# A hybrid decoder step on one core: memory K/V projected first, the SSD scan cut into items among dense tiles, key units among attention heads

## The chip, the cores and the metric

The kernel runs on one core of one Trainium2 chip. The metric is the device time of one execution in microseconds (us). Five engines work in parallel, each through its own list of instructions: TensorE (PE, matrix products and transposes), VectorE (DVE), ScalarE (ACT), GpSimd (POOL) and SyncE (SP, which here issues nearly all loads).

## What is computed

One step of one decoder layer, in fp32, with the same weights for a prompt of 256 tokens and for 32 sample tokens (8 sequences, 4 steps each); the kernel treats them as one matrix of 288 columns.

```python
def trunk_layer(h, l, q_start, conv_state, ssm_state, k_past, v_past, mem_k, mem_v, p):
    hn = rmsnorm(h, p['norm_mix'][l])
    proj = hn @ p['w_in'][l]                                  # 1024 x 4112
    z, xbc, dt_raw, q, k, v = jnp.split(proj, SPLIT_IDX, axis=-1)
    y_ssd, new_conv, new_ssm = ssd_branch(z, xbc, dt_raw, conv_state, ssm_state, ...)
    y_att = moba_attention(q, k_all, v_all, q_start, p['rel_bias'])
    h = h + jnp.concatenate([y_ssd, y_att], axis=-1) @ p['w_out'][l]
    h = h + cross_attend(rmsnorm(h, p['norm_ca'][l]), mem_k, mem_v, ...)
    hn = rmsnorm(h, p['norm_mlp'][l])
    h = h + jnp.square(jax.nn.relu(hn @ p['w_up'][l])) @ p['w_down'][l]
```

`ssd_branch` is a causal convolution over x, B and C with SiLU, a scan with 16 heads of 64 and a state of 128 (two chunks of 128 for the prompt, one chunk of 4 steps for each sample sequence, from its own stored state), a gate with SiLU(z) and a norm. `moba_attention` has 8 heads of 64; a query attends to its own block of 256 keys and to the three earlier blocks whose mean key scores highest. The sample's 1024 past keys and values per sequence are gathered from a pool by a page table. The memory's K/V (256 tokens) are projected from a normed memory input for the prompt, and read from a cache for the sample. Outputs are y of both groups and the new K/V, memory K/V, convolution and SSM states.

## The kernel before

**Tiles and blocks.** A dense projection is done in pairs of tiles: 128 output columns x 288 tokens each, 16 matmuls of one 128x128 weight tile (8 k-tiles, fp32) by 288 columns. A pair's weights are one block of 256 columns, 1 MB, in a ring of four slots (`wring`); `load_block` (L563) issues it. Tiles gather in PSUM banks 0 and 1 and are evicted by VectorE.

**Units.** The gathered cache comes in units of 2 MB, eight pages of 256 KB. `K(g,k)` and `V(g,k)` are four units for each of two groups g of four sequences. `kvring` has two slots, and `load_unit` (L587) issues one DMA a page in a register loop that reads the page number (L594 to L596). It first waits in `slot_free` until the unit two before is used. A K unit on TensorE is 32 transposes (L829) and 32 short products with the queries (L924); a V unit is 16 products (L945). `MK`/`MV` are the memory's cache units, `ST` the SSM states.

**Turns.** Every transpose into PSUM that is copied out again, and many small products, are "turns". `plan_turns` (L239) numbers them in program order over banks 2, 3 and 6 (`TURN_BANKS`); ScalarE and VectorE take them alternately. Each turn waits for the copy of the turn three before.

**The order.** `make_plan` (L109) writes one list, `SEQ`, by hand. All five engines walk the same list, each doing its own part of each item, and wait for one another by semaphores. SP walks it too, and does `load_block` at a pair and `load_unit` at a unit: one serial queue. Around the change it is: qk 0, sum of squares of x, `early` (eight transposes of the memory and its squares, the convolution history), qk 1, then K(0,0) to K(0,3) each with a pair (qk, v) behind it, own 0 (products of queries with the sample's new keys, followed by `self_bounds` on VectorE and `row_exps` on ScalarE), v 1, K(1,0), kvtok (K/V to token rows, stored), the memory's norm, four m pairs among K(1,1) to K(1,3), mtok; then `heads_in` (POOL loads the relative bias rows by DMA, VectorE adds them to the first scores), x pairs, V units and eight self heads, dt, z pairs. A head on TensorE is a product of scores (L969), a transpose of probabilities (L829) and a product with values (L980). Then a meeting of all engines, and `ssd()` alone: two prompt chunks (segments, outputs, new states), the sample's chunk with 16 state reads one by one (L1113) and 16 updates (L1132 on TensorE, L1942 on VectorE, four operations each). Then the output projection (8 k-tiles of the SSD part and 4 of the attention part, L864 and L866), caq (queries of the cross attention, L843 at 467.45 us), a meeting, the cross attention, its projection and the MLP.

**The start.** VectorE's first part makes the relative-bias tables and waits for all six table loads (`wait_ge(tab_in, 96)`) ahead of L1999. Only behind that does it evict the transposed x (L1646). SP issues the tables behind x, the vectors and weight block 0.

The lines that the prediction speaks of:

```python
            def load_block(key):
                g = BLOCK[key]
                if g >= SLOTS:
                    old = BLOCKS[g - SLOTS]
...
                    with sp.Fori(0, 8) as i:
                        page = sp.value_load(pages[0:1, ds(i + first, 1)], min_val=0, max_val=cache.shape[0] - 1)
                        sp.dma_start(big[:, ds(i * 512 + (n % 2) * 4096, 512)],
                                     cache[ds(page, 1)].rearrange("o p n -> p (o n)")).then_inc(kv_in[n % 2], 16)
```

## Time and profile before

| | |
|---|---|
| runs: median of 3 (lowest, highest) | 789.86 us (789.83, 791.85) |
| the profiled execution's own time | 791.33 us |
| its span in the profile | 789.5 us |
| mean granted TensorE clock | 0.950 of full speed |
| TensorE busy | 709.1 us (90%) |
| VectorE busy | 415.8 us (53%) |
| ScalarE busy | 142.0 us (18%) |
| POOL busy | 120.5 us (15%) |
| bytes moved | 126.18 MB, mean 160 GB/s |

The span is what the profile sees between the first and the last instruction; the own time has the launch around it. Times in the rows are from the span's start. "Busy" is the time an engine's instructions ran; matmuls are pipelined, so a busy TensorE is not one at its peak. The granted clock is a share of 2.4 GHz: at 0.5 TensorE runs at 1.2 GHz. In a timeline row, the brackets give the time for which the engine was idle before the row's first instruction, and the operation that released it.

### The profile page before, as it was taken

Reading aid. Unit: us, or ns where it says so; the run is one execution under the profiler, and the core shown is the slowest. Engines: PE = TensorE matmul, PEld = TensorE weight load, DVE = VectorE, ACT = ScalarE, POOL = GpSimd, SP = SyncE. Lnnn points to the kernel's source line nnn. Section 1 sums busy time; section 2 is a strip of 40 time slices with the busy share of each in tenths; the row PEclk is TensorE's granted clock in tenths of the full one; section 3 lists DMA queues with packets and bytes.
Section 4 is the critical chain, followed back from the end, with each engine's and each line's share of the span. In section 5 each row is a group of like instructions: output and inputs, shape, how many; then the busy total and the mean of one; then the engine's idle time right before and its main releaser. Section 6 shows DMA issues by size and latency. Waiting matters only on the chain. (4 is left out here: it accounts for less than half of the span.)

```text
span 789.5 us, 12071 instructions
## 1 busy us (share of the span) xinstructions
PE 709.1 (90%) x4351; PEld 543.4 (69%) x4351; DVE 415.8 (53%) x905; ACT 142.0 (18%) x322; POOL 120.5 (15%) x200
## 2 busy tenths in 40 slices
PE   4879999997999997889879997868999999999993
PEld 2456677785756674543326775537999999999992
DVE  2253244243876821884387222536788887445524
ACT  2131114222101021431111000411211111000002
POOL 3120001003002002200034110003254444000000
PEclk9969999999899999796979998989999999999998
DMA  9563677687779955400006790456354444544401
GB/s 285 135 178 100 207 241 254 224 264 210 220 232 288 294 142 138 137 1 1 1 0 165 235 320 0 147 174 213 108 159 145 145 150 152 186 161 161 160 1 61
DMA packets 102492, 126.18 MB, mean 160 GB/s; under 512 B 6385, under 2 KB 78565, under 8 KB 102440
## 3 DMA queue, kind: packets, MB, share of 16 engines
q1 hardware_dynamic: 99240, 115.08, 46.5%
q0 software_dynamic: 3200, 10.39, 4.6%
q8 instruction: 35, 0.57, 0.3%
q14 instruction: 17, 0.14, 0.1%
HBM read 117.14 MB, written 8.31 MB: 159 GB/s over the span
## 5 line engine op out<-in xcount | busy, mean ns | idle before, releaser
L843 PE MATMUL ps<-hw,wring 128*128 128x288 f32 x576 | 152.3, 426 | 5.7 <-DVE qs L1692 3.7
L843 PEld LDWEIGHTS ps<-hw,wring 128*128 128x128 f32 x576 | 114.5, 200 | 42.4 <-DVE qs L1692 4.1
L1646 DVE COPY tmp<-ps 128x512 f32<-128x512 f32 (+3 forms) x84 | 53.6, 643 | 67.3 <-PE ps L829 61.4
L829 PEld LDWEIGHTS ps<-ident,big 128*128 128x128 f32 x400 | 45.6, 146 | 37.2 <-issue 13.1
L829 PE MATMUL ps<-ident,big 128*128 128x128 f32 x400 | 58.6, 289 | 10.0 <-DVE tmp L1646 6.3
L1441 ACT ACTIVATE tmp<-ps 128x512 f32<-128x512 f32 (+4 forms) x71 | 39.7, 562 | 131.4 <-PE ps L829 111.3
L1239 PE MATMUL ps<-hw,wring 128*128 128x144 f32 x256 | 35.5, 294 | 2.2 <-DVE hw L1649 2.2
L709 POOL TENSOR_TENSOR acc<-acc,sq 128x288 f32<-128x288 f32 (+1 forms) x35 | 27.9, 798 | 52.9 <-ACT sq L1447 50.8
L1239 PEld LDWEIGHTS ps<-hw,wring 128*128 128x128 f32 x256 | 33.7, 196 | 2.7 <-DVE hw L1649 2.7
L1239 PE MATMUL ps<-big,wring 128*128 128x144 f32 x256 | 34.0, 286 | 0.0
L866 PE MATMUL ps<-big,wring 128*128 128x288 f32 x128 | 32.6, 408 | 0.5 <-DVE big L1649 0.5
L1239 PEld LDWEIGHTS ps<-big,wring 128*128 128x128 f32 x256 | 32.4, 190 | 0.0
L866 PEld LDWEIGHTS ps<-big,wring 128*128 128x128 f32 x128 | 24.2, 190 | 7.8 <-DVE big L1649 1.3
L843 PE MATMUL ps<-tmp,wring 128*128 128x256 f32 x128 | 28.5, 381 | 0.0
L924 PE MATMUL ps<-tmp,qs 128*32 128x256 f32 x320 | 25.6, 390 | 2.9 <-ACT tmp L1441 1.6
L758 POOL COPY attT<-ohT 64x16 f32<-64x16 f32 (+1 forms) x24 | 4.6, 194 | 150.6 <-ACT ohT L1441 141.8
L1595 ACT ACTIVATE xc<-ps 128x144 f32<-128x144 f32 x20 | 5.8, 288 | 119.5 <-PE ps L1239 119.5
L843 PEld LDWEIGHTS ps<-tmp,wring 128*128 128x128 f32 x128 | 24.1, 190 | 3.6 <-issue 0.4
L1602 ACT ACTIVATE big<-big 128x288 f32<-128x288 f32 x32 | 13.0, 444 | 74.2 <-DVE big L2113 74.2
L809 POOL TENSOR_TENSOR tmp<-big 128x144 f32<-128x144 f32 x16 | 15.9, 997 | 66.3 <-ACT big L1602 66.3
L829 PE MATMUL ps<-ident,tmp 128*128 128x128 f32 (+1 forms) x94 | 16.1, 304 | 10.0 <-DVE tmp L1772 4.7
L1239 PE MATMUL ps<-tmp 128*128 128x144 f32 x192 | 24.8, 286 | 0.0
(306 smaller groups left out, 1177.1 us busy)
## 6 DMA issues: line engine op xcount, KB each, us to landing
wring<-in_w_in SPq DMA_DIRECT2D x16, 1024.0 KB, 6.9
big<-in_cache_k SPq DMA_DIRECT2D x64, 256.0 KB, 2.7
big<-in_cache_v SPq DMA_DIRECT2D x64, 256.0 KB, 3.5
wring<-in_w_up SPq DMA_DIRECT2D x16, 1024.0 KB, 5.3
wring<-in_w_down SPq DMA_DIRECT2D x16, 1024.0 KB, 5.0
wring<-in_w_out SPq DMA_DIRECT2D x8, 768.0 KB, 8.7
wring<-in_w_ca_kv SPq DMA_DIRECT2D x4, 1024.0 KB, 5.3
big<-in_state_ssm SPq DMA_DIRECT2D x8, 512.0 KB, 6.1
```

Source lines behind the costliest of these rows:

```text
L709: pool.tensor_tensor(a, a, sq[:, m % 2, 0:n], ALU.add).then_inc(acc_done, 1)
L758: copy = pool.tensor_copy(dst, src)
L809: step(pool.tensor_tensor(ff_sums[:, 0, n], a[1], a[0], ALU.subtract))
L829: last = pe.transpose(ps[0:c, bank(key), col:col + r], in_, ident[0:r, 0:r])
L843: last = pe.matmul(ps[:, t % 2, 0:width], w, rhs(c * k_tiles + k), start=(c + k == 0), stop=(c == chunks - 1 and k == k_tiles - 1))
L866: last = pe.matmul(ps[:, t % 2, 0:T], w, z[:, k, :], start=(k == 6), stop=(k == 5))
L924: last = pe.matmul(ps[32 * b:32 * b + 32, bk, lo:lo + 256], qs[:, c, u[1] * GB + b, :], (xKT if cross else KT_)[:, step % 2, b, :], start= ...
L1239: last = pe.matmul(ps[:, bank_, col * HALF:(col + 1) * HALF], w(k), x(k), start=(start and k == 0), stop=(stop and k == 3))
L1441: act.activation(dst, src, ACT.Copy).then_inc(turn_act, 1)
L1595: act.activation(parts[:, u % 2, 0], ps[:, A, 0:HALF], ACT.Copy).then_inc(p1_made, 1)
L1602: act.activation(ff[:, c * T:(c + 1) * T], ff[:, c * T:(c + 1) * T], ACT.Square).then_inc(ff_done, 1)
L1646: dve.tensor_copy(dst, src).then_inc(turn_dve, 1)
```

## The change

It writes `SEQ` anew and adapts every engine's part to it. No product of the reference's is dropped.

- **Start**: the memory input, block x0, the convolution history and block m0 are issued by SP ahead of the tables. All engines first do the memory transposes (`memt`), the history (`hist`) and the tables (`tab`); VectorE's wait for the tables stays ahead of its x copies.
- **Dense part**: pairs of x and m come first, then dt, z, qk, v. The first m pair and the first x pair are held in PSUM until their norms are there (`HELD`).
- **Scan**: cut into `cv`, `tok`, `sums`, `seg`, `stt`, `yd`, `upd`, `ys`, `yo`, `sst`, the sample's chunk first (`CHUNKS = [2, 0, 1]`), most of them between single z, qk and v tiles. The state reads go four at a time. The square norm of y (`zsq`), `state` and the drain `over` stand between the K units.
- **Units**: K(0,0) follows all dense tiles but those of the output. The eight K units stand among seg, yo, kvtok, zsq, own, probs and heads 0 to 3; the V units among heads 4 to 7 and the SSD part of the output projection (`oz`). The attention part (`oa`) follows the last V unit. `load_unit(n + 2)` is issued at unit n.
- **Evictions**: some turns get a fixed engine (`EVICTOR`, `PLACE_OF`). Shared buffers replace some copies. One of the two meetings is gone.
- POOL loads the bias rows at `heads_in` only behind the drain; ScalarE's `zsq` waits for two K/V stores to land, since it writes where their source is.

The core of the diff:

```diff
-    pair("qk", 0, 1)
-    item("ss", 0)
-    item("early")
-    pair("qk", 1, 1)
+    item("memt")
+    item("hist")
+    item("tab")
+    pair("x", 0)
+    pair("m", 0)
+    item("ss", "x")
+    pair("x", 1)
+    item("ss", "mem")
+    pair("m", 1)
...
     unit("K", 0, 3)
+    item("heads_in", "self")
     item("own", 0)
-    pair("v", 1, 1)
     unit("K", 1, 0)
-    item("kvtok")
-    item("ss", 1)
-    pair("m", 0, 1)
+    item("ss", "ssd")
+    item("head", "self", 0)
     unit("K", 1, 1)
     item("probs", 0)
-    pair("m", 1, 1)
+    item("head", "self", 1)
...
-            load_block(BLOCKS[0])
+            sp.dma_start(memin, I["mem_prompt"].rearrange("(g p) n -> p g n", p=P)).then_inc(mem_in, 16)
+            load_block(0)
+            sp.dma_start(cvin, I["state_conv"]).then_inc(cv_in, 16)
+            load_block(1)
...
             for s in SEQ:
-                if s[0] == "pair":
-                    for c in range(s[3]):
-                        if BLOCK[s[1:3] + (c,)] >= done:
-                            load_block(s[1:3] + (c,))
-                elif s[0] == "unit":
-                    load_unit(s[1:])
...
+                elif s == ("seg", 0, 1):
+                    load_unit(2)
+                elif s == ("seg", 0, 3):
+                    load_unit(3)
+                elif s[0] == "unit" and s[1] != "ST" and UNIT[s[1:]] + 2 < len(UNITS):
+                    load_unit(UNIT[s[1:]] + 2)
...
                 elif s == ("heads_in", "self"):
-                    in_ps(pool, ("mvtok", 1))
+                    pool.wait_ge(ssd_over, 2)
+                    in_ps(pool, ("sf", 1))
                     pool.wait_ge(rb_out, 16)
                     load_bias(0), load_bias(1)
...
+                elif s[0] == "stt":
+                    for k in range(0, 20, 4):
+                        if k < 16:
+                            for i in range(k, k + 4):
+                                state_turn(i)
+                        if k == 4:
+                            pe.wait_ge(cz_made, 1)
+                        if k >= 4:
+                            for i in range(k - 4, k):
+                                turned(pe, ("state", i))
+                            for i in range(k - 4, k):
+                                state_read(i)
...
+                elif s[0] == "zsq":
+                    act.wait_ge(y_used, 4 + s[1] + 1)
+                    act.wait_ge(kst_out[0], 16)
+                    act.wait_ge(kst_out[2], 16)
+                    for c in (2 * s[1], 2 * s[1] + 1):
+                        square("ssd", c, z[:, c, :], T)
```

How the instructions move, at three places. SP at the start, before (the tables are the rows from rb to mask_p):

```order
L614 DMA vec_rows<-in_conv_w 48x128
L572 DMA wring<-in_w_in 128x8x256
L616 DMA rb<-in_rel_bias 128x1x8
L617 DMA rb_tab<-in_rel_bias 32x8
L618 DMA step_of<-in_step_of 128x4
L619 DMA big<-in_onehot_s 128x1056
L620 DMA wring<-in_onehot_p 32x512
L621 DMA wring<-in_mask_p 8x512
L622 DMA big<-in_mem_prompt 128x2x1024
L623 DMA mkv<-in_state_conv 24x1536
L572 DMA wring<-in_w_in 128x8x256 x2
```

and in the change:

```order
L743 DMA vec_rows<-in_conv_w 48x128
L744 DMA tmp<-in_mem_prompt 128x2x1024
L701 DMA wring<-in_w_in 128x8x256
L746 DMA mkv<-in_state_conv 24x1536
L701 DMA wring<-in_w_ca_kv 128x8x256
L748 DMA rb<-in_rel_bias 128x1x8
L749 DMA rb_tab<-in_rel_bias 32x8
L750 DMA step_of<-in_step_of 128x4
L751 DMA big<-in_onehot_s 128x1056
L752 DMA wring<-in_onehot_p 32x512
L753 DMA wring<-in_mask_p 8x512
L701 DMA wring<-in_w_in 128x8x256
```

The memory, the history and a second weight block now stand ahead of the tables.

TensorE at own 0, before (L843 a dense pair, L829 and L924 the next K unit, behind L1216, own 0):

```order
L843 MATMUL ps<-hw,wring 128x288 x16
L829 MATMUL ps<-ident,big 128x128 x16
L924 MATMUL ps<-tmp,qs 32x256 x4
L829 MATMUL ps<-ident,big 128x128 x8
L924 MATMUL ps<-tmp,qs 32x256 x4
L829 MATMUL ps<-ident,big 128x128 x8
L924 MATMUL ps<-tmp,qs 32x256 x8
```

and in the change (L976 and L1046 are the K units' transposes and products, L1088 the first two scores of the heads, L1338 own 0):

```order
L976 MATMUL ps<-ident,big 128x128 x8
L1046 MATMUL ps<-tmp,qs 32x256 x8
L1088 MATMUL ps<-kT,qz 128x256 x4
L1338 MATMUL ps<-kT,qs 32x32 x16
L976 MATMUL ps<-ident,big 128x128 x16
L1046 MATMUL ps<-tmp,qs 32x256 x4
L976 MATMUL ps<-ident,big 128x128 x8
L1046 MATMUL ps<-tmp,qs 32x256 x4
```

The dense pair between own 0 and K(1,0) is gone, and two score products of the heads stand ahead of own 0.

TensorE at the end of the V units, before (L945 a V unit, L843 dense tiles, L980, L829 and L969 a head, L954 pvend):

```order
L945 MATMUL ps<-big,tmp 32x512 x8
L843 MATMUL ps<-hw,wring 128x288 x16
L980 MATMUL ps<-tmp,vtok 64x256 x2
L829 MATMUL ps<-ident,tmp 128x128 x4
L969 MATMUL ps<-kT,qz 128x256 x2
L843 MATMUL ps<-hw,wring 128x288 x16
L945 MATMUL ps<-big,tmp 32x512 x8
L980 MATMUL ps<-tmp,vtok 64x256 x2
L829 MATMUL ps<-ident,tmp 128x128 x4
L843 MATMUL ps<-hw,wring 128x288 x32
L945 MATMUL ps<-big,tmp 32x512 x8
L954 MATMUL ps<-vtok,tmp 32x512 x4
```

and in the change (L1067 a V unit, L1017 dense tiles, L1107 and L976 a head, L1076 pvend):

```order
L1067 MATMUL ps<-big,tmp 32x512 x8
L1017 MATMUL ps<-big,wring 128x288 x8
L1107 MATMUL ps<-tmp,vtok 64x256 x2
L976 MATMUL ps<-ident,tmp 128x128 x4
L1067 MATMUL ps<-big,tmp 32x512 x16
L1107 MATMUL ps<-tmp,vtok 64x256 x2
L1067 MATMUL ps<-big,tmp 32x512 x8
L1076 MATMUL ps<-vtok,tmp 32x512 x4
L976 MATMUL ps<-ident,tmp 128x128 x4
L1017 MATMUL ps<-big,wring 128x288 x8
L1017 MATMUL ps<-attT,wring 128x288 x32
```

Before, the three L945 rows are V(1,1) to V(1,3), with four dense pairs and two heads among them. In the change the rows of L1067 are V(1,0) to V(1,3): one dense tile and one head stand ahead of V(1,1) and V(1,2), which follow one another (x16), and one product of the last head ahead of V(1,3). The attention part of the output stands behind.

## Rows read from the trace of the kernel before

**Rows 1.** Busy time by stretch: us, each engine's busy time (instructions), clock, DMA share, GB/s.
```profile
0.00:60.00 60.00, 40.08 (x129) 25.17 (x130) 20.50 (x43) 14.75 (x38) 14.95 (x25) 0.89 0.68 197
60.00:311.00 251.00, 240.74 (x1476) 170.00 (x1474) 118.08 (x262) 49.08 (x108) 18.19 (x43) 0.99 0.71 215
311.00:419.50 108.50, 90.13 (x389) 42.56 (x388) 71.99 (x162) 27.75 (x52) 13.86 (x31) 0.84 0.13 39
419.50:467.50 48.00, 47.45 (x197) 36.72 (x196) 18.50 (x40) 5.67 (x11) 13.85 (x17) 1.00 0.83 263
467.50:549.00 81.50, 65.09 (x351) 45.08 (x349) 34.27 (x74) 18.17 (x47) 7.86 (x16) 0.92 0.41 137
549.00:774.00 225.00, 222.36 (x1794) 221.50 (x1794) 146.05 (x318) 20.71 (x55) 50.15 (x65) 0.99 0.43 138
774.00:789.50 15.50, 3.21 (x24) 2.38 (x24) 6.37 (x10) 5.89 (x12) 1.63 (x3) 0.75 0.21 77
```

**Rows 2.** Timeline of the start: start us, us, engine, line, operation [idle before, releaser].
```profile
13.27 0.29 DVE L1999 TENSOR_TENSOR wring<-rb,step_of 128x128 f32<-128x128 f32 x1 [13.27 <-DMA wring<-in_mask_p]
...
26.29 10.29 PE L843 MATMUL ps<-hw,wring 128*128 128x288 f32 x32 [2.00 <-DVE wring L2012]
...
38.24 1.95 DVE L1726 RECIPROCAL rstd<-rstd 128x288 f32<-128x288 f32 x1 [0.60 <-ACT rstd L1539]
...
45.67 1.41 PE L829 MATMUL ps<-ident,big 128*128 128x128 f32 x4 [0.59 <-DVE tmp L1646]
...
47.76 1.44 PE L829 MATMUL ps<-ident,mkv 24*128 24x24 f32 x12 [0.69 <-DVE tmp L1646]
...
49.14 10.81 PE L843 MATMUL ps<-hw,wring 128*128 128x288 f32 x32
```

**Rows 3.** Busy time by stretch, two short stretches.
```profile
8.00:22.00 14.00, 10.71 (x29) 5.40 (x30) 6.56 (x13) 6.28 (x14) 5.97 (x8) 1.00 1.07 335
...
495.00:515.00 20.00, 17.01 (x154) 10.47 (x154) 11.46 (x24) 8.29 (x24) 0.00 (x0) 1.00 0.51 178
```

**Rows 4.** Timeline, K(0,0) and its next dense pair; own 0's bounds beside a pair.
```profile
59.78 1.47 PE L829 MATMUL ps<-ident,big 128*128 128x128 f32 x12
...
67.21 8.03 PE L843 MATMUL ps<-hw,wring 128*128 128x288 f32 x32
...
111.19 8.03 PE L843 MATMUL ps<-hw,wring 128*128 128x288 f32 x32
...
111.60 1.23 DVE L1737 TENSOR_REDUCE small<-ps 128x4 f32<-128x1024 f32 x1
...
119.62 0.18 ACT L1460 ACTIVATION_READ_ACCUMULATOR tmp<-tmp,small 128x1 f32 x1
```

**Rows 5.** Timeline of the heads and V units.
```profile
182.89 2.17 POOL L721 DMA_DIRECT2D tmp<-bias_rows  x4
...
192.03 0.69 DVE L1963 SCALAR_TENSOR_TENSOR tmp<-ps,tmp 128x512 f32<-128x512 f32 x1 [10.73 <-DMA tmp<-bias_rows]
...
211.03 10.83 SPq L596 DMA_DIRECT2D big<-in_cache_v  x8
...
212.35 7.92 PE L843 MATMUL ps<-hw,wring 128*128 128x288 f32 x32
...
220.20 1.92 PE L945 MATMUL ps<-big,tmp 128*32 128x512 f32 x16
```

**Rows 6.** Timeline of the scan: transposes, two state reads, the updates.
```profile
359.74 2.79 PE L829 MATMUL ps<-ident,big 128*128 128x128 f32 x12 [0.28 <-issue]
...
372.14 1.05 PE L1113 MATMUL ps<-tmp 128*32 128x512 f32 x2
...
373.70 1.04 PE L1113 MATMUL ps<-tmp 128*32 128x512 f32 x2
...
400.42 18.35 PE L1132 MATMUL ps<-tmp 128*128 128x512 f32 x28 [3.43 <-DVE big L1942]
```

**Rows 7.** DMA issues: tile and source, operation, count, KB each, median us to landing.
```profile
big<-in_cache_v SPq DMA_DIRECT2D x64, 256.0 KB, 3.5
```

More of the change, by code:

```diff
@@ L110, in make_plan, with pair, tile @@
     seq = []
-    def pair(kind, n, chunks):
-        seq.append(("pair", kind, n, chunks))
+    def pair(kind, n):
+        seq.append(("tile", kind, n, 0))
+        seq.append(("tile", kind, n, 1))
+    def tile(kind, n, half):
+        seq.append(("tile", kind, n, half))
     def unit(*a):
@@ L119, in item @@
         seq.append(a)
-    pair("qk", 0, 1)
-    item("ss", 0)
-    item("early")
-    pair("qk", 1, 1)
-    unit("K", 0, 0)
-    pair("qk", 2, 1)
-    unit("K", 0, 1)
-    pair("qk", 3, 1)
+    item("memt")
[7 more added lines that the diff above has]
+    pair("m", 1)
+    pair("x", 2)
+    unit("ST", 0)
+    unit("ST", 1)
+    pair("m", 2)
+    pair("x", 3)
+    pair("m", 3)
+    pair("x", 4)
+    item("mtok")
@@ new lines, in make_plan @@
+    pair("x", 5)
+    item("dt")
+    tile("z", 0, 0)
+    item("dt_series")
+    tile("z", 0, 1)
+    item("dt_rates")
+    tile("z", 1, 0)
+    item("silu_x")
+    tile("z", 1, 1)
+    tile("z", 2, 0)
+    item("cv")
+    item("tok", 2)
+    tile("z", 2, 1)
+    item("sums", 2)
+    tile("z", 3, 0)
+    item("seg", 2, 0)
+    item("stt")
+    tile("z", 3, 1)
+    item("silu_z")
+    item("yd")
+    item("upd", 0, 2)
+    tile("qk", 0, 0)
+    item("ys")
+    item("upd", 2, 6)
+    tile("qk", 0, 1)
@@ new lines, in make_plan @@
+    item("upd", 6, 10)
+    item("tok", 0)
+    tile("qk", 1, 0)
+    item("upd", 10, 14)
+    tile("qk", 1, 1)
+    item("upd", 14, 16)
+    item("sums", 0)
+    tile("qk", 2, 0)
+    item("seg", 0, 0)
+    tile("qk", 2, 1)
+    item("seg", 0, 1)
+    item("yo", 0, 0)
+    tile("qk", 3, 0)
+    item("seg", 0, 2)
+    item("yo", 0, 1)
+    tile("qk", 3, 1)
+    item("seg", 0, 3)
+    item("yo", 0, 2)
+    tile("v", 0, 0)
+    item("yo", 0, 3)
+    item("sst", 0)
+    item("tok", 1)
+    tile("v", 0, 1)
@@ L129, in make_plan @@
+    item("sums", 1)
+    tile("v", 1, 0)
+    item("seg", 1, 0)
+    tile("v", 1, 1)
+    item("seg", 1, 1)
+    item("yo", 1, 0)
+    unit("K", 0, 0)
+    item("seg", 1, 2)
+    item("yo", 1, 1)
+    item("kvtok", 0, 2)
+    item("seg", 1, 3)
+    item("yo", 1, 2)
+    unit("K", 0, 1)
+    item("yo", 1, 3)
+    item("sst", 1)
+    item("kvtok", 2, 3)
+    item("zsq", 0)
+    item("zsq", 1)
     unit("K", 0, 2)
-    pair("v", 0, 1)
+    item("zsq", 2)
+    item("zsq", 3)
+    item("state")
+    item("over")
@@ L219 @@
     elif s[0] == "dt":
         TILE["dt"] = len(TILE)
-    elif s[0] == "unit" and s[1] in ("K", "V"):
-        UNIT[s[1:]] = len(UNIT)
-    elif s[0] == "ssd":
-        for h in range(2):
-            UNIT[("ST", h)] = len(UNIT)
     elif s[0] == "unit":
         UNIT[s[1:]] = len(UNIT)
-N_BLOCKS, N_TILES, N_USED = len(BLOCK), len(TILE), len(USED)
+N_BLOCKS, N_TILES = len(BLOCK), len(TILE)
+HELD = {("x", 0): "x", ("m", 0): "mem", ("caq", 0): "ca"}
+EVICT, BANK, IN_BANK = {}, {}, {}
+for s in SEQ:
+    if s[0] == "tile" and s[1:3] not in HELD:
+        EVICT[s[1:4]] = len(EVICT)
+    elif s[0] == "dt":
+        EVICT["dt"] = len(EVICT)
+    elif s[0] == "ss":
+        for kind, name in HELD.items():
+            if name == s[1]:
+                for half in range(2):
+                    EVICT[kind + (half,)] = len(EVICT)
@@ L1529, in _ @@
+            leave("vec")
+            for c in range(DT):
+                leave(("x", c))
+                turned(act, ("x", c))
+                square("x", c, h3[:, c, :], T)
             for s in SEQ:
```

1390 lines of the change are left out of this document (703 added, 687 removed).

## The prediction

> **What bounds the kernel now.** I read the busy time by stretches first [rows 1]: TensorE is busy for 709.07 us of the 789.50 us span (the sum of the seven rows), so the kernel is bound by TensorE, and what can change is its idle time and the time it spends at the lower of its two clock levels. Both are concentrated: 18.4 us idle in the scan stretch 311.00 to 419.50, with a mean granted clock of 0.84; 19.9 us idle in the first 60 us at 0.89; 16.4 us around the meeting before the cross attention; 12.3 us at the end. In 60 to 311, where every K or V unit is followed by dense tiles, only 10.3 of 251.0 us are idle. The DMA engines move 39 GB/s during the scan against 215 and 263 GB/s beside it. So spreading the scan among dense tiles could pay at most for what the scan stretch loses. But the dense tiles it uses are the ones that covered the K units and the page loads. The question is what is late next once that cover has moved. I walk TensorE's order from 0 to the start of caq0 at 467.45; behind it both orders are the same, and I leave its 322.05 us of span unchanged.
>
> **The start.** Today mask_p, the last table, lands at 13.27, and VectorE, which stands in a wait for it ahead of everything, begins then [rows 2]. In the changed order 1 MB of the memory, 1 MB of weights beyond today's and the 0.15 MB convolution history (0.1 MB more of smaller pieces) are issued ahead of the tables. The DMA engines deliver 335 GB/s with a share of 1.07 from 8 to 22 us [rows 3], so 2.25 MB are 6.7 us: mask_p lands at about 20. Nothing hides this, since the x columns wait in PSUM for VectorE. The eight memory transposes now precede the first tile; today they run at 2.1 us for two chunks (45.67 to 47.76), so 8.2 us, and the conv history 1.4 us plus 0.9 us for its copies. First tile: 26.29 + 6.7 + 8.2 + 2.3 = 43.5. Today's same pieces stood between 36.4 and 49.14, partly behind a 1.95 us reciprocal. Then x0 (10.3), m0 (7.0), the sum of squares (0.7), some 4 us in which TensorE waits for root, reciprocal and eviction, and 2.9 us for the lower clock: x1 begins at 68.4.
>
> **Tiles with the scan among them.** A dense pair costs 7.85 us in a full-clock stretch ([rows 5], 212.35 to the unit at 220.20), one on 256 columns 6.9. Five x pairs, three m pairs, mtok, dt, four z pairs, four qk pairs and two v pairs are 39.0 + 20.7 + 1.9 + 3.9 + 31.2 + 31.2 + 15.6 = 143.5 us. The scan is mostly moved, and two parts get cheaper. The 16 state reads follow one another every 1.56 us [rows 6]: 25 us. In fours, four states are turned while the four before are copied, and their eight products stand together as a V unit's sixteen do, which take 1.92 us [rows 5]: 16 turns at 0.49 (1.47 for three, [rows 4]) and four groups at 0.96 are 11.7 us. The updates (18.35 us for 28 products, paced by four 343 ns VectorE operations each, whose end TensorE waits for) are spread among tiles and are then TensorE's own 15.7 us. With the other scan items that precede the first K unit this part is 53.5 us. VectorE does not bound: its 118.08 us from 60 to 311 and 71.99 us in the scan stretch [rows 1] spread over the 430 us from 68 to 498. Waits at item borders, about 5 us (ten or so of 0.5 us). The first K unit begins at 68.4 + 143.5 + 53.5 + 5 = 270.4. Loads are no bound here: 17 weight blocks, the states and two K units, 25 MB, are 75 us at the rate shown.
>
> **K units without dense tiles.** From here I count from the first K unit. Eight units at 7.4 to 7.5 us are 60 us (59.78 to 67.21 [rows 4]). The small items between them (segments and outputs of the second chunk, kvtok, own, sums, probs, three heads at 2.37) are 26.8 us. Now the waits:
> - ahead of K(0,2), 6.0 us: ScalarE's squares of z wait for a store of token rows to land (counted like a page, 3.5 us [rows 7]), and POOL adds them at its own pace. Today the norm of y stands in the scan stretch.
> - ahead of K(0,3), 5.2 us: the last squares, state and the drain.
> - ahead of K(1,0), 10.0 us: own 0 is today followed by a dense v pair of 8.03 us, during which VectorE works on the bounds from 111.60 on and ScalarE exponentiates until 119.80; TensorE does not notice [rows 4]. In the new order K(1,0) follows at once, and its copies stand behind those 8.2 us (111.60 to 119.80) on VectorE and ScalarE. Besides, the heads' bias loads are issued by POOL behind the scan's last work; issue to use is 9.1 us today (182.89 to 192.03 [rows 5]).
> - ahead of K(1,1), 5.9 us: sum of squares, table load, root and a reciprocal like the 1.95 us one [rows 2], with only a head beside it.
>
> Together 27.1 us. After each stall TensorE runs for a while at its lower level: a tile pair right behind an idle stretch took 10.29 or 10.81 us where 8.03 us is the usual time [rows 2, 4]. For K units I take about 2.2 us a stall and a little more at the longest, 9.9 us. The last K unit ends at 60 + 26.8 + 27.1 + 9.9 = 123.8.
>
> **V units and the page loads.** A unit's eight page DMAs occupy SP for 10.83 us [rows 5], one unit after another in SP's queue, and a page lands 3.5 us after issue [rows 7]. Today a head of 2.37, a dense pair and the unit itself, 212.35 to 222.12, are 12.1 us from one unit to the next, and the queue keeps up. In the new order 14 of the 16 loads fall behind the first K unit, and each waits for the unit two before it. V(0,1) is loaded when K(1,3) is done, at 123.8; from then seven loads follow one another: 7 x 10.8 + 1.2 for weight issues = 76.8. TensorE has less than that in between (heads of 2.37, V units of 1.92, three dense pairs), so it waits 6.9 us ahead of V(0,3), 8.2 ahead of V(1,2), 7.9 ahead of V(1,3), which ends at 123.8 + 76.8 + 3.5 + 1.9 = 206.0. Then pvend (2.4), oz (3.9) and the four attention k-tiles of every output pair (15.6): 228.1.
>
> **The sum.** 270.4 + 228.1 = 498.5 against 467.45 is +31.05 us: span 820.6. The profiled execution took 791.33 us for its 789.5 us of span, so it would be 822.4; the median of the runs shown is 789.86, 1.47 under the profiled one, so 821. Per stage: start +6.7, K stretch some 37 us of waits and lower clock, V stretch 23, and against them the scan stretch's 18.4 us of idle and its lower clock, 18 us of cheaper reads and updates, and some of the 7 and 8 us of today's idle.
>
> **Weighed against a rule.** The rate of 335 GB/s is the row's. The Trainium skill, "DMA: Bandwidth & Descriptors", on measured bandwidth, gives 341 GB/s for 1 MB transfers; by that a load of 2 MB would be 6.15 us, and if the hardware alone set the pace the V stretch would have no wait. This case's rows show 10.83 us of issue for 2 MB, so here the queue's issue, and not the engines, is the limit.
>
> **Bounds of what today's trace does not show.** The K stretch's waits: nothing (everything is ready ahead), up to 27.1 + 8 if both stand behind one another. Loads per unit: 10.8 as today, 12.4 with weights among them as a few units show, or only the landing if SP runs ahead. Reads in fours: a gain of 0 to 18 us. I take the middle in each, since the nearest rows are of the same instructions.
>
> **Rivals.**
> A, **the K stretch is covered** (the other side, faster): the squares, the bounds and the norm are ready before TensorE asks. Then the loads alone set the end: K(0,3)'s load starts at 23.4, thirteen loads x 10.8 + 1.2 end at 165.0, and + 3.5 + 1.9 + 2.4 + 3.9 + 15.6 = 192.3. With the first K unit at 262 to 270 caq0 begins at 454 to 462: 776 to 785. It decides from the point where the stretch's waits and clock loss, 37 us in my walk, come to under about 5 us. For it: today's stretch 60 to 311 has hardly any wait. Against it: there every unit has a dense pair beside it. 0.20.
> B, **the page loads are no limit** (SP gets ahead, or issues faster when it waits for nothing): the 23 us of V waits go, 798. Against it: 10.8 us whenever it has free run. 0.15.
> C, **the lower clock stays**: the K stretch is nearly all transposes and short products. At the low level twelve transposes took 2.79 us (359.74) against 1.47 (59.78) [rows 4, 6]. If the level does not come back, a K unit loses 5.8 us in place of 2.0, over six units +23: 844. Against it: 495.00 to 515.00, which is memory units and heads, has a granted clock of 1.00 [rows 3]. The Trainium skill, "TensorE: Matmul & The Clock Gate", Part 4, says that transposes do not count as activity for the clock; in that window it was 1.00 although many of its 154 matmuls were transposes, which speaks against the rule's strict reading. 0.15.
> D, **the gains and the waits cancel**, 787.5 to 792.2: 0.04.
>
> **How the numbers follow.** My forecast, 812 to 831 by itself, has 0.46. Faster by over 0.3% (2.4 us, about what a measurement of this kernel can tell from no change) has A's 0.20; same 0.04; slower 0.76. The range takes in B and C, and the upper half of A: 781 to 845.
>
> **What would show it.** mask_p landing at 20 and not 13; first tile at 43.5; first K unit near 270; waits of TensorE of about 6, 5, 10 and 6 us ahead of K(0,2), K(0,3), K(1,0), K(1,1), released by ScalarE and VectorE; SP's page loads back to back with V(0,3), V(1,2), V(1,3) released by a DMA; caq0 at 498. I am wrong if K(1,0) does not wait, if SP issues a unit in well under 10 us, or if the scan's pieces among the tiles bring waits that sum to more than 10 us.

## The result, and the profile after

The changed kernel takes 838.66 us (median of 4 runs, 837.75 to 841.35) against 790.16 us before (4 runs, 789.83 to 791.85): ratio 1.0615, 95% interval 1.0585 to 1.0645. That is 48.5 us slower. The forecast was 821, or 31 us slower. The profiled execution took 839.43 us for a span of 837.6 us.

Busy time by stretch of the changed kernel, with the same columns as [rows 1]. The stretches are: the start up to the first pair of evicted x tiles, tiles with the scan among them, from the first K unit to the first V unit, the V units, the attention part of the output, then the same three as before (the meeting and the cross attention's first part, the rest, the end):

```profile
0.00:64.00 64.00, 36.54 (x128) 23.11 (x128) 17.89 (x40) 12.94 (x29) 14.97 (x25) 0.97 0.50 152
64.00:275.40 211.40, 208.84 (x928) 148.03 (x928) 118.26 (x284) 30.20 (x44) 15.08 (x34) 0.95 0.52 152
275.40:398.30 122.90, 90.99 (x737) 58.04 (x735) 62.13 (x114) 40.03 (x87) 19.54 (x30) 0.86 0.54 152
398.30:498.00 99.70, 71.02 (x334) 38.60 (x334) 24.20 (x59) 9.01 (x30) 5.07 (x20) 0.79 0.71 211
498.00:513.50 15.50, 15.50 (x65) 12.16 (x64) 6.69 (x16) 3.10 (x7) 5.07 (x7) 1.00 0.61 204
513.50:595.00 81.50, 65.47 (x348) 45.60 (x348) 29.50 (x66) 19.52 (x47) 7.21 (x16) 0.92 0.31 102
595.00:822.00 227.00, 223.29 (x1799) 221.88 (x1797) 149.58 (x324) 21.20 (x56) 50.93 (x66) 0.99 0.43 140
822.00:837.60 15.60, 3.17 (x24) 2.33 (x24) 6.20 (x9) 5.89 (x12) 1.61 (x3) 0.68 0.21 77
```

The scan has found its cover: from 64 to 275.4 TensorE is idle for 2.6 us, and the scan stretch of [rows 1] with its 18.4 us of idle no longer exists. But the next two stretches have 31.9 and 28.7 us of idle, and granted clocks of 0.86 and 0.79. Ahead of caq0 TensorE was idle for 49.1 us before and is idle for 90.6 us now. Over the whole span its busy time rises by 5.8 us (709.07 to 714.83), though it has the same 4351 instructions, and though the state reads now cost it less (e2: 12.5 us for the item instead of 24.2). The mean granted clock fell from 0.950 to 0.923. An estimate from these numbers: without the cheaper reads the busy time would be up by 5.8 and 11.7 us, so the lower clock costs some 17 us. The idle time of TensorE rises by 42.3 us. Busy and idle time together are the 48.1 us of span.

**The start.** Timeline rows that answer to [rows 2]:

```profile
19.75 0.29 DVE L2112 TENSOR_TENSOR wring<-rb,step_of 128x128 f32<-128x128 f32 x1 [19.75 <-DMA wring<-in_mask_p]
...
41.83 9.72 PE L1017 MATMUL ps<-hw,wring 128*128 128x288 f32 x32 [2.10 <-DVE wring L2132]
...
61.33 1.95 DVE L1847 RECIPROCAL rstd<-rstd 128x288 f32<-128x288 f32 x1 [19.56 <-ACT rstd L1630]
...
63.90 10.92 PE L1017 MATMUL ps<-hw,wring 128*128 128x288 f32 x32 [4.96 <-DVE tmp L1804]
```

The last table lands 6.5 us later than before, and VectorE waits for it with all of x behind it.

**The K units.** TensorE's rows with a long wait from K(0,2) to K(1,1), answering to [rows 4, 5]. The row at 323.14 is the transposes of the final state, ahead of K(0,3):

```profile
309.74 1.11 PE L976 MATMUL ps<-ident,big 128*128 128x128 f32 x4 [5.66 <-DVE tmp L1772]
...
323.14 1.97 PE L976 MATMUL ps<-ident,tmp 128*128 128x128 f32 x8 [5.54 <-DVE tmp L2048]
324.90 3.62 PE L976 MATMUL ps<-ident,big 128*128 128x128 f32 x16
...
335.31 0.90 PE L1338 MATMUL ps<-kT,qs 128*32 128x32 f32 x32
336.14 1.35 PE L976 MATMUL ps<-ident,big 128*128 128x128 f32 x8
338.65 0.66 PE L976 MATMUL ps<-ident,big 128*128 128x128 f32 x4 [1.16 <-DVE own_raw L1772]
347.43 1.11 PE L976 MATMUL ps<-ident,big 128*128 128x128 f32 x4 [8.13 <-ACT tmp L1551]
348.48 1.08 PE L1046 MATMUL ps<-tmp,qs 128*32 128x256 f32 x8
...
353.73 0.64 PE L1046 MATMUL ps<-tmp,qs 128*32 128x256 f32 x8
...
361.06 1.11 PE L976 MATMUL ps<-ident,big 128*128 128x128 f32 x4 [3.32 <-DVE tmp L1772]
```

Before, own 0 (L1338 now) had a dense pair behind it. Now K(1,0)'s transposes follow at once, fill the three banks and wait until VectorE's bounds and ScalarE's exponentials are through. After a wait four transposes take 1.11 us instead of 0.66, and a group of products 1.08 instead of 0.64; by 353.73 the full rate is back.

What holds K(0,2) is on ScalarE, POOL and VectorE:

```profile
302.25 0.68 DVE L1772 COPY sq<-ps 32x512 f32<-32x512 f32 x1 [0.60 <-PE ps L982]
...
303.22 0.53 POOL L829 DMA_DIRECT2D out_sample_k<-sq  x1 [12.64 <-DVE sq L1772]
...
305.96 0.78 ACT L1557 ACTIVATE sq<-big 128x288 f32<-128x288 f32 x2 [2.69 <-DMA out_sample_k<-sq]
```

The square of z goes into the buffer from which the sample's K rows are being stored.

**The V units.** SP's own queue, from the end of the K loads on (each `big<-in_cache_v x8` is one unit; the row at 396.03 is the first page of V(0,1) by itself, out of the row above it):

```profile
384.15 34.68 SPq L725 DMA_DIRECT2D big<-in_cache_v  x24
396.03 0.35 SPq L725 DMA_DIRECT2D big<-in_cache_v  x1
419.06 0.40 SPq L701 DMA_DIRECT2D wring<-in_w_out  x1
420.43 10.88 SPq L725 DMA_DIRECT2D big<-in_cache_v  x8
431.54 0.40 SPq L701 DMA_DIRECT2D wring<-in_w_out  x1
432.89 24.91 SPq L725 DMA_DIRECT2D big<-in_cache_v  x16
458.02 0.40 SPq L701 DMA_DIRECT2D wring<-in_w_out  x1
459.38 22.79 SPq L725 DMA_DIRECT2D big<-in_cache_v  x16
```

and the waits of TensorE, in all, for the whole kernel:

```profile
PE ps L1067 <- DMA big<-in_cache_v: 26.4, 4, 10.3
PE ps L976 <- DVE tmp L1772: 17.0, 11, 5.7
PE ps L976 <- ACT tmp L1551: 11.3, 3, 8.1
```

SP is hardly free from 384.15 to 482.17, and four of the eight V units wait for their pages, 26.4 us in sum.

A row's length is easily misread. Issuing one page takes 0.35 us, and the next page's issue begins about 1.5 us after this one's. A row of eight pages, 10.88 us, thus holds seven intervals of 1.50 us and one issue of 0.35 us. To the first page of the next unit it is another interval: 12.0 us a unit, and not 10.88. The row of 10.83 us in the kernel before [rows 5] reads the same way; its first two pages begin at 211.03 and 212.55.

### The profile page after: what moved, and what is told of

It is laid out like the page before. It is cut to its first block and busy times, and to the rows that moved or that the text cites. A ratio compares the mean times of both kernels' runs of the same rounds, so it can differ in the third digit from the quotient of the medians.

```text
span 837.6 us, 12069 instructions
## 1 busy us (share of the span) xinstructions
PE 714.8 (85%) x4351; PEld 549.8 (66%) x4351; DVE 414.5 (49%) x908; ACT 141.9 (17%) x312; POOL 119.5 (14%) x199
## 5 line engine op out<-in xcount | busy, mean ns | idle before, releaser
L1017 PE MATMUL ps<-hw,wring 128*128 128x288 f32 x576 | 158.0, 435 | 11.9 <-DVE tmp L1804 5.0
L1017 PEld LDWEIGHTS ps<-hw,wring 128*128 128x128 f32 x576 | 116.4, 205 | 52.7 <-issue 5.8
L976 PE MATMUL ps<-ident,big 128*128 128x128 f32 x384 | 61.2, 308 | 28.1 <-DVE tmp L1772 14.9
L976 PEld LDWEIGHTS ps<-ident,big 128*128 128x128 f32 x384 | 48.1, 157 | 48.1 <-DVE tmp L1772 20.1
L1772 DVE COPY tmp<-ps 128x512 f32<-128x512 f32 (+4 forms) x73 | 48.1, 667 | 57.1 <-PE ps L976 55.0
L1551 ACT ACTIVATE tmp<-ps 128x512 f32<-128x512 f32 (+3 forms) x77 | 42.8, 564 | 163.8 <-PE ps L976 79.7
L1067 PE MATMUL ps<-big,tmp 128*32 128x512 f32 x160 | 24.3, 735 | 26.4 <-DMA big<-in_cache_v 26.4
L1017 PE MATMUL ps<-big,wring 128*128 128x288 f32 x128 | 35.1, 435 | 0.0
L1017 PE MATMUL ps<-attT,wring 128*128 128x288 f32 x128 | 33.0, 420 | 1.9 <-POOL attT L902 1.9
L976 PE MATMUL ps<-ident,tmp 128*128 128x128 f32 (+1 forms) x110 | 22.8, 343 | 13.8 <-DVE tmp L1893 5.7
L1017 PEld LDWEIGHTS ps<-big,wring 128*128 128x128 f32 x128 | 25.9, 206 | 11.4 <-issue 4.2
L1046 PE MATMUL ps<-tmp,qs 128*32 128x256 f32 x320 | 29.2, 440 | 3.3 <-ACT tmp L1551 2.3
L976 PEld LDWEIGHTS ps<-ident,tmp 128*128 128x128 f32 (+1 forms) x110 | 14.8, 168 | 25.2 <-DVE tmp L1893 9.0
L1017 PEld LDWEIGHTS ps<-attT,wring 128*128 128x128 f32 x128 | 25.2, 198 | 9.3 <-issue 2.1
L1067 PEld LDWEIGHTS ps<-big,tmp 128*32 128x32 f32 x160 | 4.7, 124 | 38.4 <-DMA big<-in_cache_v 29.2
L1017 PE MATMUL ps<-tmp,wring 128*128 128x256 f32 x128 | 28.3, 379 | 0.0
L1017 PEld LDWEIGHTS ps<-tmp,wring 128*128 128x128 f32 x128 | 24.3, 190 | 3.5
```

What stands on the lines that cost most here:

```text
L976: last = pe.transpose(ps[0:c, bank(key), col:col + r], in_, ident[0:r, 0:r])
L1017: last = pe.matmul(ps[:, BANK[key], 0:width], w, rhs, start=(k == 0), stop=(k == K_TILES[kind] - 1))
L1046: last = pe.matmul(ps[32 * b:32 * b + 32, bk, lo:lo + 256], qs[:, c, u[1] * GB + b, :], KT_[:, step % 2, b, :], start=(c == 0), stop=(c == 3),
L1067: last = pe.matmul(ps[32 * b:32 * b + 32, 7, :], (xPT if cross else PT)[:, col, 32 * b:32 * b + 32], src[:, b, t, :], start=(first and t = ...
L1551: act.activation(dst, src, ACT.Copy).then_inc(turn_act, 1)
L1772: dve.tensor_copy(dst, src).then_inc(turn_dve, 1)
```

## The experiments

All but three start from the changed kernel. "Against before" is the median less that of the runs of the kernel before on the same chip (788.99, 788.12 and 787.08 us in the three sets). The change itself stands at +48.5, by its own set of runs; it was not run again beside the experiments. Single runs of the kernel before spread from 781.8 to 793.2 us in these sets, so differences of 2 or 3 us between medians are at the edge, and I read the traces beside them.

**Tables ahead of the memory (e1).**

```diff
-            sp.dma_start(memin, ...)
             load_block(0)
-            sp.dma_start(cvin, ...)
-            load_block(1)
             sp.dma_start(rb4[:, :], ...)
...
             sp.dma_start(mask_p, I["mask_p"]).then_inc(tab_in, 16)
+            sp.dma_start(memin, ...)
+            sp.dma_start(cvin, ...)
+            load_block(1)
             load_block(2)
```

> The change with SP's order of loads at the start as before: block x0, the tables, then the memory, the history and block m0. Theory (the start is a wait of VectorE for the last table): mask_p lands at 13.3 us and not 19.75, the first dense tile begins at about 35.4 and not 41.8, and all behind it moves by the same, 838.7 - 6.5 = 832. Rival (what counts is when the memory and block m0 are there): their later landing gives the gain back, 836 to 839.

Measured: 832.42 us, +43.4 against before. mask_p lands at 13.28, the first tile begins at 34.71, the first K unit at 267.61 instead of 275.41, and the span is 829.8 us, 7.8 less. The late table is a link of the chain, and its price comes through to the end: TensorE's idle time over the span is 6.2 us less than in the change (116.6 instead of 122.8), nearly the 6.5 us by which the table is earlier, and its busy time is 1.6 us less.

**State reads one by one (e2).** The four-at-a-time loop undone, a turn and the read of two turns before in alternation.

```diff
-                    for k in range(0, 20, 4):
...
-                            for i in range(k - 4, k):
-                                state_read(i)
+                    state_turn(0)
+                    state_turn(1)
+                    pe.wait_ge(cz_made, 1)
+                    for k in range(16):
+                        if k + 2 < 16:
+                            state_turn(k + 2)
+                        turned(pe, ("state", k))
+                        state_read(k)
```

> The change with its 16 state reads one by one (a turn, then the read of two turns before), as in the kernel before, and nothing else undone. Theory (the reads in fours save their own time on TensorE and nothing hides them): the item takes about 25 us instead of 12.5, the first K unit begins 12 to 13 us later and the end too: 851, 849 to 853. Rival (something else, such as the copies of the turns, paces this item, or later waits absorb it): 838 to 844.

Measured: 845.12 us, +58.0 against before, so 9.5 us more than the change. From the item's first row to the next dense tile are 24.2 us (164.98 to 189.16) instead of 12.5 (165.40 to 177.89). The first K unit begins at 285.20, 9.8 us later. The time lies between the theory's 849 to 853 and the rival's 838 to 844. The reads in fours are a real gain: 11.7 us where they stand, of which 9.8 are left at the first K unit; from 160 to 200 us the granted clock is 1.00 here and 0.91 in the change. What reaches the end is less sure: 9.5 us by the differences to the kernel before, but 5.0 by the two profiled spans (842.6 and 837.6 us). Behind the first K unit TensorE is busy for 7.5 us less here than in the change (461.95 and 469.43 us), with the same instructions and a granted clock of 0.92 against 0.91.

**Fixed page numbers (e3).** The register loop on SP is gone, and the gather with it.

```diff
-                    with sp.Fori(0, 8) as i:
-                        page = sp.value_load(pages[0:1, ds(i + first, 1)], ...)
-                        sp.dma_start(big[:, ds(i * 512 + (n % 2) * 4096, 512)],
-                                     cache[ds(page, 1)].rearrange("o p n -> p (o n)")).then_inc(kv_in[n % 2], 16)
+                    for i in range(8):
+                        sp.dma_start(kvring[:, n % 2].rearrange("p b a n -> p (b a) n")[:, i, :],
+                                     cache[first + i:first + i + 1].rearrange("o p n -> p (o n)"))...
```

> The change with fixed page numbers: the page table is not read and pages 0 to 63 are loaded in place of the listed ones, without the register loop; the same bytes in the same order, so the gather is left out. Theory (SP's issue of 1.36 to 1.5 us a page paces the V units): issue falls to some 0.4 us a page, the waits of TensorE for cache_v (26.4 us) go to under 3 us, and with them most of the lower clock there: about 805, 800 to 812. The K stretch's four waits of 5.7, 5.5, 8.1 and 3.3 us stay as they are. Rival (the DMA engines or the landing of 2 MB pace them): a unit still takes 9 us or more, and the time is 825 or above.

Measured: 812.77 us, +23.8 against before. SP's queue and the one wait of a V unit that is left long:

```profile
383.42 22.37 SPq L724 DMA_DIRECT2D big<-in_cache_v  x24
408.38 0.38 SPq L701 DMA_DIRECT2D wring<-in_w_out  x1
412.72 3.67 SPq L724 DMA_DIRECT2D big<-in_cache_v  x8
...
442.54 12.31 SPq L724 DMA_DIRECT2D big<-in_cache_v  x16
450.07 4.78 SPq L724 DMA_DIRECT2D big<-in_cache_v  x8
...
459.25 3.50 PE L1066 MATMUL ps<-big,tmp 128*32 128x512 f32 x16 [6.05 <-DMA big<-in_cache_v]
```

Where SP has nothing queued ahead, a unit is issued in 3.67 us, a page every 0.47 us, against 10.88 us and 1.50 us with the loop. V(1,2) and V(1,3) still take 12.31 us together, but that is not the rate of the transfers: the row at 450.07 is V(1,3) by itself, and SP waits for it until V(1,1), which had its slot, is used (448.08 to 450.00 on TensorE). V(1,3) then begins at 459.25, 9.2 us behind its first issue, and that is the 6.05 us of wait. The waits for cache_v fall from 26.4 to 6.3 us, where under 3 were expected, and the attention part of the output begins at 469.07 instead of 498.03. The K stretch's waits stay: 5.5, 5.5, 8.1, 3.3 us. So SP's issue, and not the bytes, paced the V units, although the time is just above the 800 to 812 of the theory. This is the largest single item of the loss: 24.7 us by the medians, 26.0 by the spans, of which 18.5 are idle time of TensorE and 7.5 its busy time, at a mean clock of 0.938 instead of 0.923.

**Half of the V pages on another queue (e6).** The same question with the gather kept: ScalarE's queue issues pages 4 to 7 of six V units.

```diff
+                elif s[0] == "unit" and s[1] == "V" and UNIT[s[1:]] + 2 in SHARED:
+                    load_half(UNIT[s[1:]] + 2)
```

> The change with the pages 4 to 7 of six V units (V(0,2) to V(1,3)) issued by ScalarE's queue and 0 to 3 by SP. Theory (issue paces the V stretch): a unit is issued in about 6 us instead of 11.6 to 12.5, the waits for cache_v fall from 26.4 to under 5 us, 838.7 - 22 - some 5 for the clock = about 812, less what the heads lose because ScalarE is blocked for some 5.5 us a unit: 808 to 820. Rival (transfer or landing paces them): 830 or above.

Measured: 819.39 us, +30.4 against before, inside the expectation at its upper end. The waits for cache_v are 8.8 us, where under 5 were expected. The two queues together give 18 of the 24.7 us.

**oz 0 beside own 0 (e4).**

```diff
     unit("K", 0, 3)
+    item("ss", "ssd")
     item("heads_in", "self")
     item("own", 0)
+    pair("oz", 0)
     unit("K", 1, 0)
-    item("ss", "ssd")
...
     unit("V", 0, 0)
-    pair("oz", 0)
```

> The change with the first output pair oz 0 moved from between V(0,0) and V(0,1) to between own 0 and K(1,0), with the sum of squares it needs ahead of own 0. Theory (the V stretch is bound by SP's issue, counted from the end of K(1,3)): the pair fills the 9.3 us wait ahead of K(1,0), so K(1,3) ends 1 to 4 us earlier (no cold clock), the V waits grow by what left the stretch, and the time falls by 1 to 4 us: 835 to 838. Rival (waits cost what they show and the pair's 8 us are saved): 829 to 831.

Measured: 833.30 us, +44.3 against before, 4.2 less than the change, just beyond the upper end of the theory and far from the rival's 8.

```profile
335.35 0.90 PE L1338 MATMUL ps<-kT,qs 128*32 128x32 f32 x32
336.18 8.03 PE L1017 MATMUL ps<-big,wring 128*128 128x288 f32 x32
344.05 1.47 PE L976 MATMUL ps<-ident,big 128*128 128x128 f32 x12
349.64 1.11 PE L976 MATMUL ps<-ident,big 128*128 128x128 f32 x4 [4.12 <-DVE tmp L1772]
```

The pair of 8.03 us fills the wait, and a smaller one (4.12 us, VectorE evicting) opens behind it. The wait ahead of K(1,1) falls from 5.0 to 2.3 us, since its sum of squares has moved too. own 1, the end of the K stretch, comes 2.8 us earlier (392.24 instead of 395.02). The waits for cache_v stay at 26.8 us, and a head now waits 4.62 us, although the V stretch has 8 us less work. V(1,3) begins 2.9 us earlier (481.61 instead of 484.55), as much as own 1 and no more: up to there the stretch was set by SP. Another 3.3 us of the span's 6.2 come behind V(1,3), at a higher clock: the last tile of oz takes 4.05 us instead of 6.29.

**The sample's token rows earlier (e5).**

```diff
     unit("K", 0, 1)
+    item("kvtok", 2, 3)
     item("yo", 1, 3)
     item("sst", 1)
-    item("kvtok", 2, 3)
```

> The change with the sample's token rows (kvtok 2) moved ahead of the last output and the states of the second chunk, behind K(0,1). Theory (the 5.7 us wait ahead of K(0,2)'s copies is ScalarE's wait for that store to land, and it is passed on to the end): the store is issued some 2.9 us earlier, the wait falls to about 3 us, the time by 3: 835.5. Rival (POOL's sums of squares or the y columns hold the copies anyway, or the V stretch takes it back): 838 to 839.

Measured: 831.77 us, +43.7 against before, 4.8 less than the change where 3 was expected. The wait ahead of K(0,2)'s copies falls from 5.66 to 2.95 us. But TensorE's idle time over the whole span has not changed (123.0 us, 122.8 in the change): the shorter wait is made up by small ones elsewhere. All of the 8.8 us by which the span is shorter is busy time (705.8 instead of 714.8 us), at a mean granted clock of 0.934 against 0.923. Part of this can be read where the wait is: behind 2.95 us of idle the next rows run at the full rate (0.66 and 0.64 us), and behind 5.66 us they took 1.11 and 1.08. But the wait ahead of K(1,1) is 3.32 us in both, and the transposes behind it take 0.66 us here and 1.11 in the change. How much of the rest is the edit's, and how much differs from run to run anyway, no run shows.

**The kernel before, with the dense pair taken from own 0 (e7).** One part of the change alone, in the other kernel.

```diff
+    pair("v", 1, 1)
     unit("K", 0, 3)
     item("own", 0)
-    pair("v", 1, 1)
     unit("K", 1, 0)
```

> The kernel BEFORE with one thing moved: the dense pair v 1 stands ahead of K(0,3) and no longer between own 0 and K(1,0). Theory (the dense pair was the cover of own 0's bounds and exponentials): TensorE waits 8 to 9.3 us ahead of K(1,0) and runs 2 to 3 us behind it at the lower clock, all of it kept to the end: 799 to 802. Rival (the cover is not needed, or later slack takes it back): 790 to 792.

Measured: 799.86 us, +11.7 against before, ratio 1.0125 (1.0074 to 1.0175).

```profile
117.03 0.87 PE L1216 MATMUL ps<-kT,qs 128*32 128x32 f32 x32
117.84 1.53 PE L829 MATMUL ps<-ident,big 128*128 128x128 f32 x12
126.97 1.12 PE L829 MATMUL ps<-ident,big 128*128 128x128 f32 x4 [7.61 <-ACT tmp L1441]
128.02 1.08 PE L924 MATMUL ps<-tmp,qs 128*32 128x256 f32 x8
```

The same wait and the same slow rows behind it appear in the kernel before as soon as the pair is gone. Moving one pair past one K unit and own 0 costs about 1%.

**The kernel before, x copied ahead of the tables (e8), and the tables midway (e10).**

```diff
-            dve.wait_ge(tab_in, 16 * 6)
-            dve.tensor_tensor(rbx..., ALU.mult).then_inc(rbx_made, 1)
             leave("vec")
...
                 scale_tile(hw[:, c, :], h3[:, c, :], "norm_mix", c, hw_done)
+                if c == 4:
+                    dve.wait_ge(tab_in, 16 * 6)
+                    dve.tensor_tensor(rbx..., ALU.mult).then_inc(rbx_made, 1)
```

(e10; in e8 the two stand behind the loop over all eight chunks.)

> The kernel BEFORE with VectorE's wait for the tables behind its copies of x instead of ahead of them. Theory (the start waits for the last table although x and the identity are there at 8.3 us): the x chain begins at 8.6 and not 13.3 us, first dense tile at 21.5 to 22 instead of 26.3, the time 4.5 lower: 785 to 786. Rival (weight block 0 or the table products then hold the first tile): 788 to 790.

Measured: 787.92 us, ratio 0.9983 (0.9950 to 1.0016): no difference that can be told, and the theory's 4.5 us missed. TensorE of e8:

```profile
17.02 4.02 PE L1157 MATMUL ps<-big,wring 128*128 128x512 f32 x6 [1.88 <-DVE wring L2005]
20.97 1.87 PE L1158 MATMUL ps<-wring,rb_tab 32*8 32x512 f32 x2
24.84 1.81 PE L843 MATMUL ps<-hw,wring 128*128 128x288 f32 x3 [2.00 <-DVE wring L2012]
```

The x chain is earlier, but the table product now stands behind all of it on VectorE, and TensorE waits for it: the first tile gains 1.45 us. Hence e10:

> The kernel BEFORE with VectorE's wait for the tables and the product behind it placed after the fifth of the eight x chunks. In e8 they stood behind all eight, so the table matmuls on TensorE (4.05 us) no longer ran beside the copies and the first dense tile came only 1.4 us earlier. Theory: x chain from 9.2 us, the product is ready at about 13.6, the table matmuls run as TensorE ends its x transposes, first dense tile at 22 and the time 4 to 4.5 us below before, ratio 0.994 to 0.995. Rival (the gain at the start is lost in the waits behind the first tile): ratio 0.998 to 1.001.

Measured over five rounds: 784.60 us against 787.08, ratio 0.9961 (0.9938 to 0.9985).

```profile
14.09 0.28 DVE L2006 TENSOR_TENSOR wring<-rb,step_of 128x128 f32<-128x128 f32 x1
...
15.39 3.75 PE L1157 MATMUL ps<-big,wring 128*128 128x512 f32 x6
19.07 1.02 PE L1158 MATMUL ps<-wring,rb_tab 32*8 32x512 f32 x2
...
22.09 9.71 PE L843 MATMUL ps<-hw,wring 128*128 128x288 f32 x32 [2.00 <-DVE wring L2013]
```

The first tile begins at 22.09 instead of 26.29. By the medians 2.5 of those 4.2 us reach the end, where 4 to 4.5 were expected; the interval holds 1.2 to 4.9, so neither can be told from the other. It is the fastest version of this study, 0.4% below the kernel before.

**The change with four repairs (e9).** x ahead of the tables, e4, e5 and e6 together.

> The change with four repairs together: x copied ahead of the wait for the tables (the wait stands at the table item, behind the memory transposes; SP's order as in the change), kvtok 2 early, oz 0 beside own 0, half of the V pages from ScalarE's queue. If the stalls are independent links of one chain: 838.7 - 10 (first tile at 31 to 32 instead of 41.8) - 3 - 4.5 - 20 = about 801, 796 to 806. If they cover one another (removing one lets another appear): 810 or above.

Measured: 803.07 us, +14.9 against before, ratio 1.0187 (1.0126 to 1.0247). First tile at 33.41; waits for cache_v 11.9 us. The repairs add up nearly as independent links of one chain (801 expected), take back 33.6 of the 48.5 us, and still leave the new order slower. TensorE is busy for 703.9 us, less than the 709.1 before, and idle for 95.3 us where it was 80.4. Of its waits there remain 2.95, 5.53 and 4.12 us in the K stretch, 4.3 us for a head, and the 11.9 us.

## Why the prediction was right or wrong

The direction, the mechanism and the places were right, and the time lay in the range of 781 to 845. But that range was wide because it took in the rivals. The forecast's own 812 to 831 was missed: 838.66 us is 17.7 above its point of 821, and nearer to the 844 of rival C, whose mechanism did not happen. So the sum was too small, mostly in one term, the V stretch. By its own steps, in spans:

| step | forecast | measured |
|---|---|---|
| last table lands | 20 | 19.75 |
| first dense tile | 43.5 | 41.83 |
| second x pair begins | 68.4 | 63.90 |
| first K unit begins | 270.4 | 275.41 |
| waits ahead of K(0,2), K(0,3), K(1,0), K(1,1) | 6.0, 5.2, 10.0, 5.9 | 5.7, 5.5, 9.3, 5.0 |
| last K unit ends, from the first | 123.8 | 119.6 |
| from there to caq0 | 104.3 | 118.5 |
| waits of V units for pages | 23.0 | 26.4 |
| caq0 begins | 498.5 | 513.55 |
| caq0 to the end | 322.05 | 324.05 |

**The start** was right. The copies of x waited for the last table, and the sum over rate gave its landing to 0.3 us. e1 shows that the wait is paid in full.

**Tiles with the scan among them** came 6.6 us longer than forecast: 211.5 us against 202.0, of which 2.9 had been booked to the start. The gain from the reads was right (12.5 us for the item, 11.7 forecast; e2). TensorE has next to no idle time there. What I left out is the lower clock around the updates, which I took to cost only their own time:

```profile
197.67 6.71 PE L1017 MATMUL ps<-hw,wring 128*128 128x288 f32 x16
...
219.90 5.84 PE L1017 MATMUL ps<-hw,wring 128*128 128x288 f32 x16
```

A dense tile has 4.05 us at the full level. The four at 185.77 (5.84), 197.67, 211.33 (4.94) and 219.90 are 7.1 us over that, about what this part came out longer. They stand among the updates, which use 32 rows of the array, and hardly any wait is near; from 200 to 215 us the granted clock is 0.79 with TensorE busy for 13.94 of the 15 us. That the updates are the cause was not tested.

**The K stretch** was right wait by wait: 27.1 us forecast, 25.5 measured. e7 shows the largest of them by itself, e5 what holds the first, and in e4 the wait ahead of K(1,1) shrinks when the sum of squares moves. The cause of the wait ahead of K(0,3) was read from the rows alone. My allowance for the lower clock, 9.9 us, was about right: the rows behind the four waits add up to 11.0 us over their full rate. The stretch ended 4.2 us early since the waits were 1.6 us shorter, and the units and small items took 83.1 us without waits and clock, where I had 86.8.

**The V stretch** is the term that was mis-sized: from the last K unit to caq0 118.5 us, where I had 104.3. The mechanism, "seven loads follow one another", is what SP's rows show and what e3, e6 and e4 confirm from three sides. What was too small is the time of a unit in SP's queue. I took the row of 10.83 us [rows 5] for a whole unit, but it ends with the last page's issue of 0.35 us and leaves out the interval to the next page: a unit counts 12.0 us. From the first page of V(0,1) at 396.03 to the end of the last row at 482.17, seven units took 86.1 us, where I had 76.8. Six units that count 12.0 and a last one of 10.9 are 82.9; the three weight issues add 1.3 (from the last page before one to the first page behind it 1.93 us instead of 1.50), as forecast; and V(1,1) took 1.72 us a page instead of 1.50, another 1.8, and did so in e4 and e5 too (24.91 and 24.90 us for the same two units), for a reason that no run shows. The 12.4 us a unit of my own bounds was the better reading. The other 5 us of the 14.2 are mainly the lower clock behind the last wait: V(1,3) took 3.64 us instead of 1.92, pvend's products 1.93 instead of 1.06, and the last output tile 6.29 instead of 4.05, with a granted clock of 0.56 from 484 to 498 us. A start of the queue's seven units 1.0 us later and a landing 1.1 us shorter than forecast cancel. The terms of this stretch, added again, give 227.9 and not 228.1, which changes nothing.

**The rivals.** A (the K stretch is covered) did not happen. B (loads are no limit) is refuted by e3, and its price is now known: I gave 23 us, the medians give 24.7, clock included. C (the lower clock stays) did not happen either, since the rows at 353.73 and later run at the full rate between waits. But its direction was right: the K and V stretches as a whole had 0.86 and 0.79, and part of what the forecast lacked is clock. The Trainium skill's rule that transposes do not count as activity ("TensorE: Matmul & The Clock Gate", Part 4) would, read strictly, have kept K(1,0) at the low level from 347.43 on. This trace does not bear that out, since the full rate returned by 353.73, but it does not settle it either: short products (L1046) stand among the transposes (L976). e5 is the closer case: there 24 transposes follow one another from 319.81 on, and the last sixteen take 2.56 us, where sixteen took 3.62 in the change at mostly the low level and 2.04 in e7 at the full one. The Trainium skill's 341 GB/s for a transfer of 1 MB ("DMA: Bandwidth & Descriptors", Bandwidth) describes the engines, not this loop: the V stretch moves 211 GB/s. In e3, with the loop gone, stretches of 6 us from 385, 404 and 430 us on moved 333, 354 and 361 GB/s.

**Where the expected gain of the change went.** It was had: the scan's idle is gone, and the reads cost half. It was then given back three times: at the start (e1: 5.1 us by the medians, 7.8 by the spans), in the K stretch (25.5 us of waits, and 11.0 of clock behind them), and at SP's queue (e3: 24.7 us). The dense tiles that now cover the scan were the cover of the K units' neighbours and the time in which SP caught up.

What stays open: how much of the busy time that e5 and e4 save is their doing and how much is the clock's own spread from run to run, whether the updates are what lowers the clock among the tiles, why one V unit was issued more slowly than the others, and the cause of the wait ahead of K(0,3).

## What to carry to other kernels

Before moving dense work to cover one stall, list what it covers where it stands: here each pair stood beside a VectorE and ScalarE chain (own 0: 8.2 us) and beside 12 us of SP's issue, and taking one pair from own 0 cost 11.7 us by itself (e7). For a queue that issues in a loop, take the interval from one start to the next (1.50 us a page here), not the length of a merged row, multiply it by the number of transfers left and compare that with the compute left at the same point; it is a bound of its own, and neither the DMA share (0.71) nor GB/s (211) shows it. And a wait for a late table ahead of unrelated copies is worth moving, but to the middle and not to the end: whoever uses its result then waits in turn (e8 against e10).

## What the runs showed of the hardware

- With a page number read from a register in a loop, SP issues a page load of 256 KB every 1.50 us (10.88 us for eight, of which the last issue is 0.35), in one unit every 1.72 us. With fixed addresses it is one every 0.47 us (3.67 for eight). On ScalarE's queue the same loop took 4.65 to 5.13 us for four pages, one every 1.4 to 1.6 us.
- After a wait of 5 to 10 us TensorE's rows take 1.7 to 1.9 times their usual time (four transposes 1.11 against 0.66 us, sixteen V products 3.64 against 1.92). After waits of 3 to 4 us both were seen: 1.11 us in the change and 0.66 in e5 behind the same 3.32 us, 1.11 in e4 and 0.66 in e9 behind the same 4.12 us. With transposes and short products alone the full rate came back about 6 us later (347.43 to 353.73).
- Two state-read products alone take 1.05 us. Eight of them for four states, placed in the four column groups of the array, also took only 1.04 to 1.06 us.
- The same kernel before had medians of 790.16, 788.99, 788.12 and 787.08 us in four sets of runs, and single runs from 781.8 to 793.2: 1.4%, far above the 0.3% that I had named as what can be told from no change.
